# LRU gates on Trainium2: two full-array matmuls of a block-diagonal weight against two 64-row matmuls side by side

## What is computed

```python
def block_diag(x, w, b):                       # 16 blocks of 64 channels
    xr = x.reshape(B, T, N_LRU_BLOCKS, LRU_BLOCK)
    return jnp.einsum('btnc,ncd->btnd', xr, w).reshape(B, T, D_LRU) + b

def rg_lru(x, h_prev, w_a, b_a, w_i, b_i, lam):
    r = sigmoid(block_diag(x, w_a, b_a))
    i = sigmoid(block_diag(x, w_i, b_i))
    log_a = -LRU_C * r * softplus(-lam)
    a = exp(log_a)
    bterm = sqrt(-expm1(2.0 * log_a)) * i * x
    h[t] = a[t] * h[t-1] + bterm[t]            # an associative scan over positions
```

## Time and profile before

| | |
|---|---|
| median of 3 runs | 1863.9 us (1859.0 to 1868.57) |
| profiled execution | 1856.7 us |
| its span | 1854.9 us |
| mean granted TensorE clock | 0.991 |
| busy: TensorE, VectorE, ScalarE, GpSimd | 1801.8, 750.4, 585.3, 546.3 us |
| LRU gate weights, 8 loads | 128 KB each, 2.0 us from issue to landing |

### The profile page before, as it was taken

The page is one execution under the profiler, slowest core; times in us unless marked ns, Lnnn a source line. Parts: engine busy times, 40 slices in busy tenths (PEclk is TensorE's granted clock), DMA queues, the critical chain, the costliest instruction groups (busy, mean ns, idle before and its releaser), DMA issues.

```text
span 1854.9 us, 29879 instructions
## 1 busy us (share of the span) xinstructions
PE 1801.8 (97%) x11240; PEld 1753.0 (95%) x11240; DVE 750.4 (40%) x1391; ACT 585.3 (32%) x1152; POOL 546.3 (29%) x320
## 2 busy tenths in 40 slices
PE   3999999999999999999998999999999999999999
PEld 3998888899999999999897999999999999999999
DVE  6605757721246666111546444411444411444411
ACT  4325534410147766111214333300333300333300
POOL 4422111122233232333225333322333322333322
PEclk9999989999999999999998999999999999999999
DMA  3111000011111111111310111111111111111113
GB/s 129 35 35 39 27 24 23 24 49 46 46 49 40 38 50 37 46 45 45 140 46 23 46 45 45 45 46 46 45 45 45 46 45 45 45 45 45 45 45 118
DMA packets 28517, 89.24 MB, mean 48 GB/s; under 512 B 3473, under 2 KB 8497, under 8 KB 28465
## 3 DMA queue, kind: packets, MB, share of 16 engines
q1 hardware_dynamic: 25488, 82.78, 13.9%
q10 hardware_dynamic: 2976, 5.72, 0.9%
HBM read 83.74 MB, written 4.75 MB: 48 GB/s over the span
## 4 chain that ended last, share of the span: by engine, by line
PE 91%; DVE 3%; ACT 2%; issue 1%; POOL 1%; DMA 0%; ACTq 0%; POOLq 0%; DVEq 0%; SPq 0%
PE banks L413 83%; PE banks L543 2%; PE banks L558 2%; PE banks L532 1%; PE banks L499 1%; PE banks L509 1%; ACT x_hi L752 1%; PE banks L662 1%; PE banks L661 1%; POOL x_lo L387 1%; DVE merged L1097 0%; DMA resid<-xT 0%; DVE ntmp L1077 0%; POOL w_lo L378 0%; ACT prB L810 0%
## 5 line engine op out<-in xcount | busy, mean ns | idle before, releaser
L413 PE MATMUL banks<-x_hi,w_hi 128*128 128x354 f32 (+1 forms) x2352 | 777.7, 331 | 22.3 <-POOL x_lo L387 15.3
L413 PE MATMUL banks<-x_lo,w_hi 128*128 128x354 f32 (+1 forms) x2352 | 767.7, 326 | 0.0
L413 PE MATMUL banks<-x_hi,w_lo 128*128 128x354 f32 (+1 forms) x2352 | 763.3, 325 | 0.0
L376 POOL TENSOR_SCALAR w_hi<-w_raw 128x1024 fp32r<-128x1024 f32 x140 | 166.5, 1190 | 1244.3 <-DMA w_raw<-W 1244.3
L413 PEld LDWEIGHTS banks<-x_hi,w_hi 128*128 128x128 f32 x2352 | 447.1, 190 | 27.9 <-issue 18.5
L413 PEld LDWEIGHTS banks<-x_lo,w_hi 128*128 128x128 f32 x2352 | 446.8, 190 | 3.0
L413 PEld LDWEIGHTS banks<-x_hi,w_lo 128*128 128x128 f32 x2352 | 446.3, 190 | 0.0
L378 POOL TENSOR_TENSOR w_lo<-w_raw,w_hi 128x1024 fp32r<-128x1024 f32 x140 | 342.0, 2443 | 11.7
L413 PE MATMUL banks<-act_hi,w_lo 128*128 128x354 f32 (+1 forms) x576 | 186.8, 324 | 0.0
L413 PE MATMUL banks<-act_lo,w_hi 128*128 128x354 f32 (+1 forms) x576 | 186.7, 324 | 0.0
L413 PE MATMUL banks<-act_hi,w_hi 128*128 128x354 f32 (+1 forms) x576 | 186.4, 324 | 0.0
(11 more groups left out here) (173 smaller groups left out, 1739.9 us busy)
## 6 DMA issues: line engine op xcount, KB each, us to landing
w_raw<-W SPq DMA_DIRECT2D x140, 512.0 KB, 3.5
sqsum<-xT ACTq DMA_DIRECT2D x2, 2120.0 KB, 10.4
o_yT<-resid SPq DMA_DIRECT2D x8, 530.0 KB, 5.0
resid<-xT SPq DMA_DIRECT2D x4, 708.0 KB, 6.7
resid<-xT SPq DMA_DIRECT2D x2, 704.0 KB, 11.1
wabs<-wab ACTq DMA_DIRECT2D x8, 128.0 KB, 2.0
mat<-mats SPq DMA_DIRECT2D x1, 192.0 KB, 5.8
vec<-vecs SPq DMA_DIRECT2D x1, 143.0 KB, 5.6
```

Source lines behind the costliest of these rows:

```text
L376: nc.gpsimd.tensor_scalar(w_hi[s][:, :], w_raw[s][:, :], 1.0, 0.0, ALU.mult, ALU.add).then_inc(w_hi_done, 1)
L413: last = nc.tensor.matmul(out[:, 0:cn], w[s][:, k * P:(k + 1) * P], x[:, k, cc:cc + cn], start=(k == 0 and j == 0), stop=(k == KT - 1 and ...
```

## The change

The two diagonal blocks of a gate's weights become one 64-row matrix each. `wabs` is now 128x128: on partitions 0 to 63 lie the weights of the first block of 64 channels, those of gate a in columns 0 to 63 and those of gate i in columns 64 to 127; on partitions 64 to 127 lie those of the second block, with i in columns 0 to 63 and a in columns 64 to 127. A piece's two products are now one per block: each contracts over 64 rows and gives both gates as 128 output partitions, the first block in bank 6, the second in bank 7. Gate a comes out on the partitions where it is wanted; gate i comes out on the other half, and ScalarE's tanh reads it there and writes it to its own half. For that ScalarE has four tanh on 64 partitions where it had two on 128. The bias table `b_i` is rolled by 64 rows for the same reason.

```diff
--- before.py
+++ after.py
@@ -179,7 +179,7 @@
         FI = sb("FI", [P, T])
         FS = sb("FS", [P, T])
         XC = [sb(f"XC{i}", [P, 354]) for i in range(3)]
-        wabs = sb("wabs", [P, 2, P])
+        wabs = sb("wabs", [P, P])
 
         at = [tr]
 
@@ -658,8 +658,10 @@
                 cn = CHUNKS[n][1]
                 pe.wait_ge(r_xc, j * 3 + (n + 1))
                 pe.wait_ge(r_tanh, j * 3 + (START + n))
-                nc.tensor.matmul(bank[6][:, 0:cn], wabs[:, 0, :], XC[n][:, 0:cn], start=True, stop=True)
-                nc.tensor.matmul(bank[7][:, 0:cn], wabs[:, 1, :], XC[n][:, 0:cn], start=True, stop=True).then_inc(r_ps, 1)
+                for e in range(2):
+                    of = slice(HD * e, HD * e + HD)
+                    last = nc.tensor.matmul(bank[6 + e][:, 0:cn], wabs[of, :], XC[n][of, 0:cn], start=True, stop=True)
+                last.then_inc(r_ps, 1)
 
             tile(0, 0, PAIR_R, x_hi, x_lo, x_dve, X_DVE["G0"])
             tile(1, 0, PAIR_R, x_hi, x_lo, y_dve, Y_DVE["G0"])
@@ -895,8 +897,8 @@
                           scale=0.5).then_inc(y_act, 1)
 
             def load_wab(j):
-                src = wab[j] if isinstance(j, int) else wab[bass.ds(j, 1)].rearrange("a p m n -> (a p) m n")
-                act.dma_start(wabs[:, :, :], src).then_inc(s_wab, 16)
+                src = wab[j] if isinstance(j, int) else wab[bass.ds(j, 1)].rearrange("a p n -> (a p) n")
+                act.dma_start(wabs[:, :], src).then_inc(s_wab, 16)
 
             def lru_u(j, n):
 
@@ -915,8 +917,11 @@
                 c0, cn = CHUNKS[n]
                 ck = slice(c0, c0 + cn)
                 wait(r_ps, j * 3 + (n + 1))
-                A(FA[:, ck], bank[6][:, 0:cn], ACT.Tanh, bias=halfb[:, cols(j + 2 * KT, 1)], scale=0.5)
-                A(FI[:, ck], bank[7][:, 0:cn], ACT.Tanh, bias=halfb[:, cols(j + 3 * KT, 1)], scale=0.5).then_inc(r_tanh, 1)
+                for e in range(2):
+                    here, there = slice(HD * e, HD * e + HD), slice(HD - HD * e, P - HD * e)
+                    A(FA[here, ck], bank[6 + e][here, 0:cn], ACT.Tanh, bias=halfb[here, cols(j + 2 * KT, 1)], scale=0.5)
+                    last = A(FI[here, ck], bank[6 + e][there, 0:cn], ACT.Tanh, bias=halfb[there, cols(j + 3 * KT, 1)], scale=0.5)
+                last.then_inc(r_tanh, 1)
                 wait(r_tanh, j * 3 + (START + n + 1))
 
                 A(row(resid, j, c0, cn), FA[:, ck], ACT.Tanh, bias=lamc[:, 0, cols(j, 1)], scale=lamc[:, 0, cols(j, 1)])
@@ -1456,17 +1461,18 @@
     xT = np.zeros((DM, T), f32)
     xT[:, :SEQ], xT[:, SMP:] = x["x_prompt"][0].T, x["x_sample"][0].T
 
-    wab = np.zeros((KT, P, 2, P), f32)
+    wab = np.zeros((KT, P, P), f32)
     for m, name in enumerate(("w_lru_a", "w_lru_i")):
         for j in range(KT):
             for e in range(2):
-                wab[j, HD * e:HD * e + HD, m, HD * e:HD * e + HD] = x[name][0, 2 * j + e]
+                at = HD * (m ^ e)
+                wab[j, HD * e:HD * e + HD, at:at + HD] = x[name][0, 2 * j + e]
     sink = x["attn_sink"][0]
     sink_p, sink_s = (np.repeat(np.tile(sink.reshape(4, 4), (1, DSEQ)), n, axis=0).T for n in (2, 1))
     bg = x["b_gate"][0]
     parts = dict(bg_lru=_cols(bg[:DM]), bg_att=_cols(bg[DM:]),
                  conv_w=x["w_lru_conv"][0].reshape(4, KT, P).transpose(2, 1, 0).reshape(P, -1), conv_b=_cols(x["b_lru_conv"][0]),
-                 b_a=_cols(x["b_lru_a"][0]), b_i=_cols(x["b_lru_i"][0]), lam=_cols(x["lru_lambda"][0]),
+                 b_a=_cols(x["b_lru_a"][0]), b_i=np.roll(_cols(x["b_lru_i"][0]), HD, axis=0), lam=_cols(x["lru_lambda"][0]),
                  g_mix=_cols(x["g_mix"][0]), g_ffn=_cols(x["g_ffn"][0]),
                  fconv_w=x["w_ffn_conv"][0].reshape(3, FT, P).transpose(2, 1, 0).reshape(P, -1), fconv_b=_cols(x["b_ffn_conv"][0]),
                  h0=_cols(x["state_lru_h"][0, 0]), g_q=np.tile(x["g_q"][0], 2)[:, None], g_k=np.tile(x["g_k"][0], 2)[:, None],
```

## The result

| | before | changed |
|---|---|---|
| median, range | 1863.88 us (1859.0 to 1868.57) | 1891.74 us (1887.34 to 1894.32) |
| ratio, 95% interval | | 1.0142 (1.0115 to 1.0168) |
| profiled execution, its span | 1856.7, 1854.9 us | 1894.3, 1892.5 us |

The changed kernel is 28 us slower. It was forecast 17.5 us slower, at 1881, with a range of 1868 to 1892: 1891.7 lies inside it by 0.3 us. The changed kernel run again gave 1887.95 us and a ratio of 1.0115 (1.0094 to 1.0136), 22 us.

The account below looks back on a forecast made before the run. It took TensorE (26.85 us a head) and the ScalarE-VectorE chain (26.06) as nearly equal bounds, with the chain binding after the change. 15.7 plus 1.8 for GpSimd gave 17.5 us on the 1863.9 median: 1881, range 1868 to 1892.

Parts of the forecast that it names:

- What bounds: LRU stage, one head: TensorE needs 26.85 us, the ScalarE-VectorE chain 26.06, so the chain has 0.79 us of slack.
- Gate products: TensorE in the LRU stage: a piece's two products take 1.00 us instead of 1.19, about 5 us over 24 pieces.
- Tanh: ScalarE in the LRU stage: two more tanh per piece at 0.45 us each, 2.7 us per head.
- Who pays: LRU loop becomes 28.76 us, TensorE waits 2.5 us a head; over eight heads, less slack, +15.7 us.
- GpSimd: LRU y slots: VectorE's FI*FS and GpSimd's w_hi meet, +0.3 us a head over six heads, +1.8 us.
- The rival on the clock: LRU stage: TensorE's waits bring the clock to 1.2 GHz, 12 us if unhidden, giving 1893; chance 5%.
- The rival bound by TensorE: LRU stage stays TensorE-bound if extra tanh cost under 0.13 us: 1859, 5%; with mode changes free, 1850, 2%.
- the relief by GpSimd: LRU stage: GpSimd begins at least 3.5 us before FI*FS, returning 2.5 us a head: 1865; chance 6%.

Follow-up runs that it names:

- The fillers: The kernel before plus one, three or six more 128-partition tanh per head, their output overwritten: ratios 1.0001, 1.0026 and 1.0075; stages 208.6, 213.0 and 223.0 us.

## Why the prediction was right, and where its sizes were off

*What bounds.* Right. The change's place was read from the chain between ScalarE and VectorE and not from the shares. The slack of the chain was put at 0.79 us. The fillers gave 1.1, and the split of the waits by starts rather than by idle rows gives 0.99: L910 came at 563.67 where the step behind the square (0.41) would have had it at 563.13, and the tanh at 564.69 where 0.57 behind L910 is 564.24. The idle column undercounts where instructions overlap.

*Gate products.* Right: 1.00 forecast, 0.99 measured, in pairs, and worth nothing in the changed kernel: with the old products and four tanh the stage is 231.3, with the new ones 231.9. The passes run in pairs, but the gap before them is 0.25 instead of 0.16, and the first pair lasts 0.56 where the second lasts 0.46. The Trainium skill ("TensorEngine Tiling (Array Packing)", Key Properties) says that a change of the tiling mode drains the engine. The trace agrees with that better than with the halved time alone, which would be 0.60 and not 0.99.

*Tanh.* This is the term that was mis-sized: "I take 0.45: two more per piece, 0.9 us; six per head, 2.7 us". That time goes with columns and not with partitions was right (551 ns for 64x354 against 548). The step was not: 0.56, because the starting partitions alternate. It also cost the two old tanh their overlap, so a piece is 1.23 longer, not 0.9. The unoverlapped 0.55 stood in the text as the largest price, 3.3 us a head; the measured 3.69 is above even that end, for this reason. Eight heads: 29.5 us instead of 21.6.

*Who pays.* The loop was forecast at 28.76 us and is 29.4. TensorE waits twice a head from head 1 on, but for one of the waits of head 3; 19.9 us in all, at the upper end of the 15 to 20. The wait for `d_lo` was put at 1 to 2 and is 4.5.

*GpSimd.* "They meet" was right (583.19 and 583.81). The price in the loop was not: +0.3 a head was taken, and 2.3 to 2.6 against 2.5 is hardly a change: FI*FS to `d_lo` got 0.07 us a head shorter. What was left out is the last head, where z and `d_lo` ran free before: 0.84 more in z, and TensorE's product came 2.71 us behind the start of the first `d_lo` instead of 0.57, 2.14 more. 3.0 us together.

The sum as measured: seven turns +17.6, the last head's way to `d_lo` +4.55, its `d_lo` +2.14, the first tanh 0.5 earlier: 23.8. By causes: tanh 29.5; slack -7.9 (seven turns of 1.13, as the fillers gave it); GpSimd in the loop -0.5; the last head's collision +3.0; the first tanh -0.5. That makes 23.6; 0.2 is unassigned. Beyond the forecast's 17.5 these are +7.9 for the tanh and +3.0 for the last head, against 2.4 for the slack and 2.3 for GpSimd in the loop.

*The total.* 17.5 forecast against 23.8 in the stage. The medians differ by 27.9 us, and by 22.1 in the repetition. The profiles show about 2 us of half clock right behind the stage, behind the long wait; otherwise what lies between these numbers and the stage's varies between executions, and the two medians stand on either side of it.

That 1891.7 lies inside the range is partly luck. The terms that the prediction names for it give 1859.0 + 11 = 1870 to 1868.6 + 18 + 3 = 1890; the stated range is 2 us wider at each end, and the median lies in that margin. The repetition's 1887.95 lies inside either. The mechanism was right; the stage's 23.8 is above the 21 of the highest sum named, because of the step of 0.56 and the last head.

The rival on the clock was partly right in its mechanism (half clock appears within the stage, 3.4 us of it at 628 us and 6.8 at 744) and wrong in its price there. The turn with the first is 29.4 like the others: half clock cost TensorE 1.7 us, and the wait of 1.3 to 1.4 us that it has at the next gate product in the other heads from head 1 on is missing in this one. The second lies in the last head, whose 4.55 us are made up by tanh (3.7) and z (0.8). The rival bound by TensorE fell with the step of 0.56, and the relief by GpSimd fell with the meeting.

## What to carry to other kernels

An engine at 70% of a loop may have no slack: add up the loop's chain through all engines, from one instruction to its own next instance, and take the waits for outsiders as its slack; here that was about 1 us of 27. A cheaper matmul layout that leaves results on other partitions is paid for by the engine that has to pick them up in pieces, and the pieces cost by columns, not by partitions. Price them at a full, unoverlapped instruction where neighbours start on different partitions.

## What the hardware showed beyond expectation

- ScalarE's overlap of about 0.11 us between neighbours is lost where the PSUM read or the write starts on another partition than the last one did: steps of 0.44 or 0.45 against 0.55 to 0.57 for 354 columns. One change costs as much as two, and the last PSUM read counts even if instructions without one lie between (0.71 against 0.59). Inside a piece the start of the bias changed along with that of PSUM.
- GpSimd and VectorE hold each other up by whole instructions: the scan of 2.29 us shows as 4.37 behind a w_lo, or w_hi of 1.05 as 2.54 behind a scan. Which of the two stands first decides who pays.
- Two float32 products of 64 rows and 354 columns run side by side: the passes of a pair start 0.01 us apart, and the pair of products takes 0.99 us of TensorE's time with the way into that form and back, against 1.19 for two of 128 rows.
